# The high and low parts of the second block's weights at the top of the on-chip memory, the rest of that block 22,528 bytes lower

## The reference, cut to what matters

```python
def reference(x, ...):
    x = first_block(x, ...)      # 2 x (norm, x @ w_in, three attentions, @ w_out, norm, add)
    return second_block(x, ...)

def second_block(x, ...):
    for l in range(DEPTH):       # DEPTH = 2
        x = layer_norm(ALPHA * x + 0.5 * swiglu(x, ffn1_gate[l], ffn1_up[l], ffn1_down[l]), ...)
        h = x @ w_in[l]
        y_pool = multiscale_pool(h[..., :D_POOL], ...)
        y_hgrn = head_rms_norm(hgrn2_recurrence(...), ...) * silu(g)
        x = layer_norm(ALPHA * x + concat([y_pool, y_hgrn]) @ w_out[l], ...)
        x = layer_norm(ALPHA * x + 0.5 * swiglu(x, ffn2_gate[l], ffn2_up[l], ffn2_down[l]), ...)
    return x
```

## The kernel before, in words

| tensor | first byte | end | mod 64 | mod 512 |
|---|---|---|---|---|
| xh, xl (both blocks) | 32,896 | 65,664 | 0 | 128 |
| onein_hi, onein_lo (first block, w_in) | 181,120 | 197,504 | 0 | 384 |
| oneout_hi, oneout_lo (first block, w_out) | 164,736 | 181,120 | 0 | 384 |
| two_raw | 66,208 | 88,736 | 32 | 160 |
| k2, s2, ln (second block) | 88,736 | 96,672 | 32 | - |
| two_hi | 96,672 | 107,936 | 32 | 416 |
| two_lo | 107,936 | 119,200 | 32 | 416 |
| hh1, hh2 | 119,200 | 164,256 | 32 | 416 |
| hl1, hl2 | 164,256 | 209,312 | 32 | 416 |
| topmost of the block (lbv of the mixers) | 223,712 | 223,808 | 32 | 480 |

## Time and profile before

### The profile page before, as it was taken

One profiled execution on the slowest core, in us unless ns is written; L12 is line 12 of the kernel. 1 busy time (PEld: TensorE's weight loads), 2 busy tenths in 40 slices (PEclk: granted clock), 3 DMA queues, 4 the chain that ended last, 5 costly groups with the idle time before them and its releaser, 6 DMA issues. The chain is left out here.

```text
span 2923.0 us, 36515 instructions
## 1 busy us (share of the span) xinstructions
PE 2650.1 (91%) x13196; PEld 2092.1 (72%) x13196; DVE 1474.9 (50%) x2197; ACT 810.1 (28%) x1503; POOL 774.4 (26%) x524
## 2 busy tenths in 40 slices
PE   7989879999779999897889999799999987899997
PEld 4867658777658878685668878588877765688776
DVE  4356743467464443557664433444433576644434
ACT  2145531256332210243232210222201434322201
POOL 1000120000232223307632232322241165522241
PEclk9988989989979999998999999899999898999999
DMA  5310022200122232131122332132322210232232
GB/s 192 96 36 1 16 100 87 72 1 1 58 87 98 90 107 89 53 94 38 58 71 94 93 102 96 49 96 93 102 89 68 83 62 30 72 94 93 97 103 77
DMA packets 57264, 222.16 MB, mean 76 GB/s; under 512 B 6664, under 2 KB 7816, under 8 KB 56768
## 3 DMA queue, kind: packets, MB, share of 16 engines
q1 hardware_dynamic: 56000, 214.01, 22.6%
q10 hardware_dynamic: 1152, 6.68, 0.6%
HBM read 218.51 MB, written 2.15 MB: 75 GB/s over the span
## 5 line engine op out<-in xcount | busy, mean ns | idle before, releaser
L196 PE MATMUL bank<-xh,two_hi 128*128 128x512 f32 x1856 | 748.6, 403 | 69.4 <-ACT xh L1079 53.3
L199 PE MATMUL bank<-xl,two_hi 128*128 128x512 f32 x1856 | 735.9, 401 | 9.4 <-POOL xl L1086 9.4
L197 PE MATMUL bank<-xh,two_lo 128*128 128x512 f32 x1856 | 744.1, 401 | 0.0
L165 DVE CAST two_hi<-two_raw 128x1024 fp32r<-128x1024 f32 (+1 forms) x298 | 238.2, 799 | 938.6 <-PE bank L199 936.0
L167 DVE TENSOR_TENSOR two_lo<-two_raw,two_hi 128x1024 fp32r<-128x1024 f32 (+1 forms) x298 | 496.6, 1666 | 10.2
L196 PEld LDWEIGHTS bank<-xh,two_hi 128*128 128x128 f32 x1856 | 355.4, 192 | 167.4 <-issue 57.6
L199 PEld LDWEIGHTS bank<-xl,two_hi 128*128 128x128 f32 x1856 | 352.9, 191 | 101.5 <-POOL xl L1086 16.4
L197 PEld LDWEIGHTS bank<-xh,two_lo 128*128 128x128 f32 x1856 | 355.3, 191 | 85.3 <-issue 0.5
L196 PE MATMUL bank<-hh,two_hi 128*128 128x512 f32 x704 | 278.9, 396 | 21.6 <-PEq L1264 21.6
L1129 POOL TENSOR_TENSOR up_hm<-up_sg,up_ub 128x512 f32<-128x512 f32 x88 | 116.5, 1324 | 654.4 <-ACT up_ub L1117 654.4
L197 PE MATMUL bank<-hh,two_lo 128*128 128x512 f32 x704 | 276.8, 393 | 0.0
(11 more groups left out here) (318 smaller groups left out, 3454.6 us busy)
## 6 DMA issues: line engine op xcount, KB each, us to landing
two_raw<-in_up SPq DMA_DIRECT2D x180, 512.0 KB, 3.5
two_raw<-in_down SPq DMA_DIRECT2D x64, 704.0 KB, 4.0
one_raw<-in_w_in SPq DMA_DIRECT2D x52, 512.0 KB, 3.6
two_raw<-in_w_in SPq DMA_DIRECT2D x40, 512.0 KB, 3.5
one_raw<-in_w_out SPq DMA_DIRECT2D x16, 512.0 KB, 3.5
two_raw<-in_w_out SPq DMA_DIRECT2D x16, 512.0 KB, 3.5
w<-in_w ACTq DMA_DIRECT2D x2, 2048.0 KB, 10.6
x<-in_x SPq DMA_DIRECT2D x1, 2048.0 KB, 8.3
```

Source lines behind the costliest of these rows:

```text
L165: v.tensor_copy(st.hi[:, h, 0:w], st.raw[:, r, 0:w]).then_inc(st.hi_made, 1)
L196: pe.matmul(out[:], wh, xh[:, kx, :], start=start, stop=False)
L197: pe.matmul(out[:], wl, xh[:, kx, :], start=False, stop=False)
L199: return pe.matmul(out[:], wh, xl[:, kx, :], start=False, stop=stop)
```

## The change

`allocate_parts` gets an argument `side`, and the second block's call passes "right". The first block's two calls keep the default.

```diff
-    def allocate_parts(self, ctx, tag=""):
+    def allocate_parts(self, ctx, tag="", side="left"):
-        self.hi = ctx.enter_context(self.nc.sbuf_tensor(f"{self.tag}{tag}_hi", [P, HL_RING, self.width], F32R))
-        self.lo = ctx.enter_context(self.nc.sbuf_tensor(f"{self.tag}{tag}_lo", [P, HL_RING, self.width], F32R))
+        self.hi = ctx.enter_context(self.nc.sbuf_tensor(f"{self.tag}{tag}_hi", [P, HL_RING, self.width], F32R, side=side))
+        self.lo = ctx.enter_context(self.nc.sbuf_tensor(f"{self.tag}{tag}_lo", [P, HL_RING, self.width], F32R, side=side))
...
-            kit.stream.allocate_parts(c1)
+            kit.stream.allocate_parts(c1, side="right")
```

## The result

The changed kernel takes 2937.74 us (median of 5 runs, 2933.48 to 2944.73) against 2922.73 us, a ratio of 1.0059 with a 95% interval of 1.0042 to 1.0076 (here and below the ratios are those on record; a quotient of two medians can differ from them by up to 0.002). That is 12 to 22 us slower. The range of the prediction holds the median, its direction doesn't: the forecast was no change, and what came is the slower rival B (2937 us), with one term more.

A forecast was written before the change was run, and what follows sets the result against it. The prediction took PE to bound most of the kernel, with products back to back. Its terms for PE, DVE, ACT and POOL, DMA and code were each 0, so 2923.0 + 0 gave a forecast of 2922.5 us, range 2912 to 2938.

The forecast's parts named there:

- rival B: Down phases: the period exceeds 64 bytes, so `hh`/`hl` pairs become slow; +14 us, 2937 us, chance 0.12.
- What bounds the kernel: Whole kernel: PE bounds most of its length, busy 2650 of 2923 us; only how long instructions take can matter.
- DVE's slack: Second block's split: DVE waits 936 us for PE, which would cover 3 us of longer or shorter splits.
- That the step depends on the pair of tiles, and not on the region: Second block's products: 226.7 or 233.3 ns by whether weights and moving tile agree modulo 64, not by memory region.
- Rival A: Up phases and second mixers: weights far above make `xh` pairs fast; about -32 us, 2891 us, chance 0.10.
- The addresses: `two_hi` at 218,080, `two_lo` at 206,816, both remainder 32 by 64; tensors moved down keep their remainder by 2048.
- The aside that a top at 229,376 would change the sign of everything: Weights' new place: with that top they would have remainder 0 by 64, and everything below would change sign.
- Products with `hh`/`hl`: weights 32, moving 32, fast as before: 2112 x 0 = 0: PE term of the down phases: remainders agree by 64, so no change; 0 us, at most 14 us lost.
- The argument that a loss of 16 cycles means 16 elements and so 64 bytes: Against a longer period: the 6.67 ns loss is 16 cycles, 16 float32 elements are 64 bytes, suiting period 64.
- rival C: Second block's products: the 6.7 ns comes from something else, such as ring stride; 2923 us, counted in the forecast's 0.78.
- I take no slower one than 233 ns for the `xh` pairs: PE's `xh` products: no third step in the rows, so pairs already slow lose nothing more; 0 us.
- The rule weighed: PE's reads: by the skill's pages two independent ports wait on no one, so any place costs 0; the trace disagrees.

The follow-up runs named there:

- e2: Kernel before with the second block's weights 64 bytes higher at the bottom of the block, all else at its old remainder; 2945.3 us, ratio 1.0082.
- e3: Changed kernel with 64 unused bytes above the weights' parts, so at the top with their old remainder; 2919.38 us, ratio 1.0001 to the kernel before.
- e1: No model, only float32r matmuls over 88 pairs of starts, low and top; differences 0, 32, 64, 96 bytes took 226.7, 233.3, 233.3, 234.3 ns.
- e4: Changed kernel with 352 unused bytes above the weights and 224 before the block's rest, all tiles at remainder 128; 2886.5 us, ratio 0.9877 to before.
- e6: Kernel before with 224 unused bytes before the second block's parts; 2891.09 us, ratio 0.9908 to before.
- e5: Matmuls alone with alternating starts, other types and widths; at 32 bytes 233.8 ns in step, 232.4 out of step, 227.2 where all agree.
- e8: Matmuls alone, float32r, weights 0 to 252 bytes above a fixed moving remainder in steps of 4; steps from 226.7 to 237.5 ns.

## Why the prediction was wrong, point by point

**What bounds the kernel: right.** PE, back to back, at the full clock; a change of 6.7 ns in 2112 steps and 1 ns in 5568 went into the time whole, with some 7 us at the lower clock on top in the profiled second block. DVE's slack took nothing and lost nothing.

**That the step depends on the pair of tiles, and not on the region: right.** e2 and e3 show it in the kernel, e1 by itself. Rival A, at 0.10, falls: the weights went where `onein` had been fast, and nothing got faster. Its price for fast `xh` pairs, 32 us, was sound: e4 made them fast by another way and gained 31 by the medians.

**The addresses: right.** Remainders of 32 by 64, 480 by 512, and all else unmoved by 2048. The traces have no addresses, but 234.3 and 233.3 ns are what the map has for these. The aside that a top at 229,376 would change the sign of everything is wrong by the same map: the differences would be 128 and 96 by 256, with 232.3 and 234.3 ns.

**The step that failed** is "Products with `hh`/`hl`: weights 32, moving 32, fast as before: 2112 x 0 = 0". The period was taken as 64 bytes and is 256 (e1). Under 256, `hh` at 416 and weights at 480 differ by 64, and that costs 6.7 ns. Two faults made it. The argument that a loss of 16 cycles means 16 elements and so 64 bytes reads a period out of the size of a loss; the map has losses of 2.2, 5.6, 6.6 and 7.6 ns in one period, so sizes say nothing of it. And three pairs of places, all with the 64 bit clear, can't tell periods of 64, 128 and 256 apart; I wrote this down under rival B and still gave 0.78 to the smallest (rival C in it). With the evidence at hand each of the three deserved about as much, and the two larger ones both meant slower. That rival B's 2937 us met the measured 2937.74 so closely is in part luck: B had the down phases' 14 us alone, without the 5 us of the `xh` pairs and what lay at the lower clock, and single executions scatter by as much as these.

**"I take no slower one than 233 ns for the `xh` pairs": wrong, 5 us.** Their difference went from 288 to 352, by 256 from 32 to 96, and the map has 234.3 ns there (e1, and e2 in the kernel). The bound was the slowest step in the trace; it was no bound for a difference that the trace didn't hold.

**Rival C, the ring's stride: falls.** Strides are the same in e3, e4 and e6, with steps of 233.3 and 226.7 ns.

**The rule weighed.** The rule of the Trainium skill's page "SBUF — State Buffer", section "Who interferes with whom", two independent read ports and no waiting, was no protection, as the prediction said: by it e2 to e4 would all be 2922 us, and they span 59 us.

## What to carry to other kernels

Where float32r matmuls with 512 columns run back to back, look at the step from start to start, not the mean length, and compare it between phases; if it is 233 ns in one and 227 in another, print the starts of the weights and the moving tiles and make them equal modulo 256 bytes (shown for starts at multiples of 32). One unused tensor of 224 bytes was worth 0.9% here, and one of 64 bytes ahead of the weights cost 0.8% (e2), so any small tensor ahead of the big ones can do either. Before a prediction rests on a period of addresses, write down which bits vary in the pairs that the trace has; a bit that never varies isn't excluded by anything.

## What the runs showed of the hardware that was not expected

- Float32r, 128 columns of weights and 512 moving: 226.7 to 237.5 ns from start to start at the full clock, with the starts. At multiples of 32 bytes it is the difference (weights start - moving start) modulo 256 alone, 226.7 to 234.4 ns; between them the difference doesn't decide by itself (e1, e5, e8). At the lower clock the two kinds of pairs that the kernel before has both take 0.42 to 0.43 us.
- Bfloat16 (215.8 ns) and plain float32 (429.2 ns for each pass) don't depend on the differences tried; float32r at 128 columns doesn't either (111.7 ns) (e5).
- The 226.7 ns came only where a whole run of matmuls agreed, not where each agreed with its own weights alone (e5). That the weight load of one matmul and the moving reads of another meet in the memory would fit this, and so would other pictures; none of the runs shows the mechanism, and it stays open.
